# Hyena's projection as three rounded products, its input split on GpSimd during DeltaNet's scan

## What is computed

```
u_l = modulate(x, ...) @ w_in            # columns 800 to 1568 are Hyena's
def hyena_mixer(u_lat, ...):             # 3 * 256 channels, latent tokens only
    uc = short_conv(u, conv_w, conv_b)   # 3 taps, per channel
    v, x1, x2 = split(uc)
    h = hyena_filters(...)               # 3 sine layers of a small network
    z = x1 * long_conv(v, h[0], d[0])
    return x2 * long_conv(z, h[1], d[1])
y = concatenate([gla, hyena, mamba, deltanet]) @ w_out
```

## Time and profile before

| | before |
|---|---|
| median of 3 runs (lowest, highest) | 1843.62 us (1841.35, 1844.65) |
| profiled execution | 1845.53 us |
| its span, first to last instruction | 1843.7 us |
| PE matmul busy | 1596.1 us (87%) |
| DVE busy | 1158.8 us (63%) |
| ACT busy | 880.6 us (48%) |
| POOL busy | 316.5 us (17%) |
| mean granted TensorE clock | 0.931 of 2.4 GHz |

### The profile page before, as it was taken

One profiled execution on the slowest core, in us unless ns is written; L12 is line 12 of the kernel. 1 busy time (PEld: TensorE's weight loads), 2 busy tenths in 40 slices (PEclk: granted clock), 3 DMA queues, 4 the chain that ended last, 5 costly groups with the idle time before them and its releaser, 6 DMA issues. The chain is left out here.

```text
span 1843.7 us, 20249 instructions
## 1 busy us (share of the span) xinstructions
PE 1596.1 (87%) x7651; PEld 1159.2 (63%) x7651; DVE 1158.8 (63%) x1329; ACT 880.6 (48%) x1210; POOL 316.5 (17%) x388
## 2 busy tenths in 40 slices
PE   5899999978998869999888699429999999999981
PEld 2454665457556658954358578328888888888861
DVE  3640552238354655663579723678888888888863
ACT  4240334334426546632110244318777777777752
POOL 0000320045002768110000044101001001101001
PEclk9889999988998979999898899659999999999986
DMA  9740200041003743330220432329999999999957
GB/s 375 244 168 1 92 1 0 0 144 41 0 1 104 235 120 87 98 103 0 69 90 3 172 116 92 154 106 385 380 400 397 384 397 392 381 402 398 380 196 205
DMA packets 101847, 337.02 MB, mean 183 GB/s; under 512 B 36167, under 2 KB 40906, under 8 KB 77047
## 3 DMA queue, kind: packets, MB, share of 16 engines
q1 hardware_dynamic: 91870, 310.89, 44.7%
q0 software_dynamic: 5328, 18.88, 4.2%
q10 hardware_dynamic: 4553, 5.97, 1.2%
HBM read 300.47 MB, written 35.23 MB: 182 GB/s over the span
## 5 line engine op out<-in xcount | busy, mean ns | idle before, releaser
L3116 DVE TENSOR_TENSOR w_lo<-w_raw,w_hi 128x2048 fp32r<-128x2048 f32 x192 | 438.4, 2291 | 65.4 <-ACT w_hi L3058 65.1
L3058 ACT ACTIVATE w_hi<-w_raw 128x2048 fp32r<-128x2048 f32 x192 | 368.0, 1917 | 144.3 <-PE ps L3008 134.1
L540 PE MATMUL ps<-hT,w_mixer 128*128 128x512 f32 (+1 forms) x768 | 313.1, 568 | 5.3 <-PEq L187 3.6
L540 PEld LDWEIGHTS ps<-hT,w_mixer 128*128 128x128 f32 x768 | 147.6, 194 | 159.4 <-issue 155.5
L3006 PE MATMUL ps<-w_hi,xsT_hi 128*128 128x512 f32 x512 | 202.9, 396 | 2.4 <-DVE xsT_lo L3121 2.4
L3008 PE MATMUL ps<-w_hi,xsT_lo 128*128 128x512 f32 x512 | 200.4, 391 | 0.0
L3007 PE MATMUL ps<-w_lo,xsT_hi 128*128 128x512 f32 x512 | 200.2, 391 | 0.0
L3006 PEld LDWEIGHTS ps<-w_hi,xsT_hi 128*128 128x128 f32 x512 | 96.8, 189 | 22.0 <-DVE xsT_lo L3121 2.8
L2974 POOL DMA_INDIRECT moe_sum<-y,idx_col x15 | 30.5, 2037 | 460.6 <-ACT y L3078 460.6
L3008 PEld LDWEIGHTS ps<-w_hi,xsT_lo 128*128 128x128 f32 x512 | 96.5, 189 | 20.4
L3007 PEld LDWEIGHTS ps<-w_lo,xsT_hi 128*128 128x128 f32 x512 | 96.8, 189 | 19.3
(11 more groups left out here) (501 smaller groups left out, 2868.6 us busy)
## 6 DMA issues: line engine op xcount, KB each, us to landing
w_raw<-in_moe_w_gate SPq DMA_DIRECT2D x64, 1024.0 KB, 7.0
w_raw<-in_moe_w_up SPq DMA_DIRECT2D x64, 1024.0 KB, 8.8
w_raw<-in_moe_w_down SPq DMA_DIRECT2D x64, 1024.0 KB, 8.9
w_mod_row<-in_w_mod SPq DMA_DIRECT2D x32, 512.0 KB, 5.0
w_mod<-in_w_mod SPq DMA_DIRECT2D x8, 1024.0 KB, 14.2
w_mixer<-in_w_in SPq DMA_DIRECT2D x4, 2048.0 KB, 11.8
dn_ma<-dn_ma SPq DMA_DIRECT2D x16, 512.0 KB, 3.7
dn_mT<-dn_ma SPq DMA_DIRECT2D x20, 256.0 KB, 3.4
```

Of the source, the lines that this page charges most:

```text
L540: last = nc.tensor.matmul(S.ps[:, 3 * (i % 2) + c, 0:n], S.w[:, k, b["col"]:b["col"] + P], S.hT[:, k, t0:t0 + n], start=(x == 0), stop=(x ...
L3058: nc.scalar.activation(wh[q % RING][:, :], S.raw[q % RAW][:, :], ACT.Copy).then_inc(s.hi, 1)
L3116: nc.vector.tensor_tensor(wl[q % RING][:, :], S.raw[q % RAW][:, :], wh[q % RING][:, :].bitcast(F32), ALU.subtract).then_inc(s.lo, 1)
```

## The change

Hyena's projection is computed in three rounded products. The weights of a block are split by ACT (high part, into spare columns of `w_mixer`) and DVE (low part, in place); the input is split once, by GpSimd at the end of its list in `dn_s`. The low part takes the input's place. The high part needs 8 blocks of 4 KB in each partition: two are new space, two lie in the context part of `hT`, and four in blocks 0, 1, 4 and 5 of `yT`, whose contents are stored to DRAM (`y_kept`) in `dn_s` and loaded back in `hy_f`. The new space comes from the tables: they lose the masks that no instruction reads, and six of the seven levels of each direction's level masks. The diff, cut to its core:

```diff
@@ def tables():
-        tabs["neg_" + name] = ((1.0 - m) * -BIG).astype(f)
-    levels = [] ...
-    tabs["levels_f"] = np.stack(levels, 1).reshape(P, -1)
-    tabs["levels_b"] = np.stack([m.T for m in levels], 1).reshape(P, -1)
+    far = ((j // 64 == c // 64) & (j // 32 != c // 32) & (j > c)).astype(f)
+    tabs["level_f"], tabs["level_b"] = far, far.T
-    tabs["dn_bd"] = (j // HV == (q % P) // HV).astype(f)
-    tabs["half"] = (j // HV == np.arange(2)[None, :]).astype(f)
@@ def project_conv(...):
+        QUARTERS = (0, 2, 3, 1)
+
+        def w_high(i, k):
+            return S.w_low[:, k, HY_COLS + P * (i % 2):HY_COLS + P * (i % 2) + P]
+
+        def split_high(act, i):
+            for j in QUARTERS if i == 0 else (None,):
+                if i == 0:
+                    act.wait_ge(weights[j], 16)
+                ks = slice(0, KD) if j is None else slice(2 * j, 2 * j + 2)
+                col = blocks[i]["col"]
+                nc.scalar.activation(w_high(i, ks), S.w[:, ks, col:col + P], ACT.Copy).then_inc(s.w_hi, 1)
+
+        def split_low(dve, i):
+            for x, j in enumerate(QUARTERS if i == 0 else (None,)):
+                dve.wait_ge(s.w_hi, x + 1 if i == 0 else i + 4)
+                ks = slice(0, KD) if j is None else slice(2 * j, 2 * j + 2)
+                col = blocks[i]["col"]
+                nc.vector.tensor_tensor(S.w_low[:, ks, col:col + P], S.w[:, ks, col:col + P], w_high(i, ks).bitcast(F32),
+                                        ALU.subtract).then_inc(s.w_lo, 1)
+
+        def rounded(pe, i, c, out):
+            ...
+            for x, k in enumerate([2 * j + e for j in QUARTERS for e in range(2)]):
+                if c == mine[i][0] and (i == 0 and k % 2 == 0 or x == 0):
+                    pe.wait_ge(s.w_lo, x // 2 + 1 if i == 0 else i + 4)
+                high = S.h_high[k][:, a0:a0 + 2, :]
+                low = S.h_low[:, k, t0:t0 + 512].rearrange("p (a b) -> p a b", a=2)
+                nc.tensor.matmul(out, w_high(i, k), high, start=(x == 0), stop=False)
+                nc.tensor.matmul(out, w_high(i, k), low, start=False, stop=False)
+                last = nc.tensor.matmul(out, S.w_low[:, k, col:col + P], high, start=False, stop=(x == KD - 1))
@@ tensor
+                    if weights:
+                        last = rounded(pe, i, c, S.ps[:, 3 * (i % 2) + c, :])
@@ scalar
+            if weights:
+                split_high(act, 0)
             norm.act(s, act)
...
             for i, b in enumerate(blocks):
+                if weights and i + 1 < NB:
+                    if i >= 1:
+                        act.wait_ge(s.prod, base[i])
+                    split_high(act, i + 1)
@@ vector
+            if weights:
+                split_low(dve, 0)
             norm.dve(s, dve, ch)
             side.start_dve(s, dve, ch)
             for i, b in enumerate(blocks):
+                if weights and i + 1 < NB:
+                    split_low(dve, i + 1)
@@ dn_s, sync
             for d in range(2):
                 load_blocks(sp, 1, d)
+            for j, b in enumerate(KEPT):
+                sp.dma_start(A["y_kept"][j], S.yT[:, b, :]).then_inc(s.y_kept, 16)
             for st in range(2, T):
@@ dn_s, gpsimd
+            pool.wait_ge(s.y_kept, 16 * len(KEPT))
+            for k in range(KD):
+                raw = S.hT[:, k, CTX:TOK].rearrange("p (a b) -> p a b", a=4)
+                nc.gpsimd.tensor_copy(S.h_high[k], raw).then_inc(s.h_hi, 1)
+                pool.wait_ge(s.h_hi, k + 1)
+                nc.gpsimd.tensor_tensor(S.h_low[:, k, CTX:TOK].rearrange("p (a b) -> p a b", a=4), raw,
+                                        S.h_high[k].bitcast(F32), ALU.subtract).then_inc(s.h_lo, 1)
@@ hy_f, sync, behind the loads of dft_fwd
+            for j, b in enumerate(KEPT):
+                sp.dma_start(S.yT[:, b, :], A["y_kept"][j]).then_inc(y_back, 16)
@@ hy_d, sync, at the end
+            sp.wait_ge(y_back, 16 * len(KEPT))
+KEPT = (0, 1, 4, 5)
```

More of the change, by code:

```diff
@@ L77, in tables @@
         wide["gafter_" + name] = (tabs["after_" + name] / GLA_TAU).astype(f)
-    levels = []
-    s = 1
-    while s < P:
-        m = ((j // (2 * s) == c // (2 * s)) & (j // s != c // s) & (j > c)).astype(f)
-        levels.append(m)
-        s *= 2
-    tabs["levels_f"] = np.stack(levels, 1).reshape(P, -1)
-    tabs["levels_b"] = np.stack([m.T for m in levels], 1).reshape(P, -1)
+    far = ((j // 64 == c // 64) & (j // 32 != c // 32) & (j > c)).astype(f)
+    tabs["level_f"], tabs["level_b"] = far, far.T
     gbd = (j // GLA_DK == np.arange(DG)[None, :] // HV).astype(f)
     wide["gla_bd"] = gbd
-    q = np.arange(DG)[None, :]
-    tabs["dn_bd"] = (j // HV == (q % P) // HV).astype(f)
-    tabs["half"] = (j // HV == np.arange(2)[None, :]).astype(f)
     def packed(ts):
@@ L468, in project_conv @@
     lo = [LAT_AT if x else CTX_AT for x in lat]
-    with Stage(nc, name, "zeroed prod evac centre conv_ch conv_done tok_t tok_e cm_done "
+    with Stage(nc, name, "zeroed prod evac centre conv_ch conv_done tok_t tok_e cm_done w_hi w_lo "
                          + side.sems + norm.sems) as s:
@@ L523, in to_tokens @@
                 last.then_inc(s.tok_t, 1)
+        QUARTERS = (0, 2, 3, 1)
[16 more added lines that the diff above has]
+        def rounded(pe, i, c, out):
+            out = out.rearrange("p (a b) -> p a b", a=2)
+            t0 = chunks[c][0]
+            a0 = (t0 - CTX) // CTX
+            col = blocks[i]["col"]
+            for x, k in enumerate([2 * j + e for j in QUARTERS for e in range(2)]):
[6 more added lines that the diff above has]
+                last = nc.tensor.matmul(out, S.w_low[:, k, col:col + P], high, start=False, stop=(x == KD - 1))
+            return last
         @s.block.tensor
@@ L535, in _ @@
                         norm.free(s, pe, 3 * (i % 2) + c)
-                    order = (0, 1, 4, 5, 6, 7, 2, 3) if weights else range(KD)
-                    for x, k in enumerate(order):
-                        if weights and i == 0 and c == mine[0][0] and k % 2 == 0:
-                            pe.wait_ge(weights[k // 2], 16)
+                    if weights:
+                        last = rounded(pe, i, c, S.ps[:, 3 * (i % 2) + c, :])
+                    for k in range(0 if weights else KD):
                         last = nc.tensor.matmul(S.ps[:, 3 * (i % 2) + c, 0:n], S.w[:, k, b["col"]:b["col"] + P],
-                                                S.hT[:, k, t0:t0 + n], start=(x == 0), stop=(x == KD - 1))
+                                                S.hT[:, k, t0:t0 + n], start=(k == 0), stop=(k == KD - 1))
                     last.then_inc(s.prod, 1)
@@ L1743, in deltanet @@
     with Stage(nc, "dn_s", "p5 p_sb pd tb dt rhs y yc z zc dz x tr wt ws vn qo ke kv s_new av o_out zero taken sub d_st chain "
-                           "pchain") as s:
+                           "pchain y_kept h_hi h_lo") as s:
         Pm = [plan.take(f"dn_p{d}", [P, HEADS, P]) for d in range(2)]
@@ L2010, in masked @@
                 dve.wait_ge(s.p5, n + 1)
-                off = S.t("levels_" + "fb"[d])[:, 5 * P:6 * P]
+                off = S.t("level_" + "fb"[d])
                 nc.vector.tensor_tensor(Pm[d][:, :, :], S.ps[:, b, :].rearrange("p (h c) -> p h c", c=P),
@@ L2374, in forward @@
             yield r, last
-    fwd_in = nc.alloc_semaphore("hy_fwd_in")
+    fwd_in, y_back = nc.alloc_semaphore("hy_fwd_in"), nc.alloc_semaphore("hy_y_back")
     with Stage(nc, "hy_f", "tables turn_in d_in folded taps tapped first skipped mixed even odd copied turned added_even "
@@ L2677, in _ @@
             result(1)
-    SPENT.extend([fwd_in, win_in] + S.hy_w)
+    SPENT.extend([fwd_in, win_in, y_back] + S.hy_w)
 HALF_AT = 32
+KEPT = (0, 1, 4, 5)
 def project_out(nc, S, A):
@@ L3238, in program @@
     S.tab = plan.take("tables", [P, tab.shape[1]])
+    S.spare_at = plan.at
+    plan.at += 8192
     S.pcols = plan.take("param_cols", [P, 69])
@@ L3259, in program @@
     S.w = plan.take("w_mixer", [P, KD, WCOLS])
+    S.h_low = nc.alloc_sbuf_tensor_at("hT_lo", [P, KD, TOK], F32R, offset=S.hT_at)
+    high = [nc.alloc_sbuf_tensor_at(f"hT_hi{k}", [P, 4, 256], F32R, offset=at) for k, at in
+            enumerate([S.spare_at, S.spare_at + SEQ * 4] + [S.yT_at + b * SEQ * 4 for b in KEPT])]
+    S.h_high = [x[:, :, :] for x in high] + [S.h_low[:, 4 * j:4 * j + 4, 0:CTX] for j in range(2)]
+    S.w_low = nc.alloc_sbuf_tensor_at("w_mixer_lo", [P, KD, WCOLS], F32R, offset=S.hT_at + KD * TOK * 4)
     S.stage_at = plan.at
@@ L3325, in declare @@
     A["moe_sum"] = nc.dram_tensor("moe_sum", (SEQ, D), F32, kind="Internal").ap()
+    A["y_kept"] = nc.dram_tensor("y_kept", (len(KEPT), P, SEQ), F32, kind="Internal").ap()
     A["out"] = nc.dram_tensor("out_0_dram", (1, SEQ, D), F32, kind="ExternalOutput").ap()
```

## The result

| | before | changed |
|---|---|---|
| median (lowest, highest) | 1843.62 us (1841.35, 1844.65) | 1831.43 us (1827.78, 1836.63) |
| profiled execution's span | 1843.7 us | 1828.7 us |
| ratio of the times, 95% interval | | 0.9932, 0.992 to 0.9945 |

The change makes the kernel faster by 12.2 us by the medians of five runs each. A second set of five runs, taken later on (e11_after_again), gave 1834.4 against 1844.97 (ratio 0.9953, 0.9939 to 0.9967), 10.6 us. The forecast was 15.0 less, 1828.6. The two profiled executions lie exactly 15.0 us apart, but that is chance, as will be seen.

What follows compares the result with a forecast made beforehand. PE was taken to bound Hyena's projection stage. Stage -12.8, tables -2.5 and GpSimd's sharing with DVE +0.3 sum to -15.0 us, so 1828.6 us against the median of 1843.6; range 1825.5 to 1834.5.

Steps and rivals of the forecast that it cites:

- PE bounds the stage; a cheaper matmul counts in full: Hyena's projection lasts as long as PE's instructions, so cheaper matmuls save their full difference unless something new makes PE wait.
- the prediction's sign of being wrong: PE's idle time before a block's first product named after DVE's weight split, or the barrier before the projection awaiting GpSimd.
- 2.96 us a block: Projection blocks: 48 rounded matmuls at 0.2267 us, 10.88 us instead of 13.84; -14.8 us for blocks 1 to 5.
- The first block, +2.0 (+0.8 to +3.2): Projection's block 0: weight splits delay DeltaNet's norm, PE idles about 3 us, block 1 starts 2.0 us later.
- Splits of later blocks hidden: Projection blocks 1 to 5: splits keep ahead of PE, cover 1.5 to 3 us; rival of late splits 0.08.
- GpSimd's split of the input costs nothing; 0.3 for sharing with DVE: DeltaNet's scan: GpSimd splits the input in idle time, done at 773 to 797 us; DVE's waits cost 0.3 us.
- The rival of a GpSimd that ends the scan: Barrier before the projection waits for GpSimd if a pair costs over 8.9 us; 1852.8 us at 10; chance 0.04.
- Stores and loads back cost nothing: Four finished blocks, 2.1 MB, stored in a pause of SP's queue and loaded back later: nothing, stores at most 5.2 us.
- The tables, -2.5: First stage, bound by bytes: 1.05 MB less at 402 GB/s saves 2.5 us (0 to 2.6); no-gain rival 0.07.
- The sum, -15.0: Whole kernel: projection stage -12.8, tables -2.5, sharing with DVE +0.3, giving 1828.6 us against the median; chance 0.70.

Runs made afterwards that it cites:

- e11_after_again: The changed kernel run again with no edit, a second set of five runs: 1834.4 us, ratio 0.9953 to the kernel before.
- e2_norm_first: Changed kernel with ACT's and DVE's split of block 0's last weight quarter moved behind the norm's first operations: 1829.09 us, ratio to before 0.9914.
- e8_halves: The kernel of e2_norm_first with GpSimd's product of gate and weight in two halves of 1024 elements: 1825.43 us, ratio to before 0.9908.
- e7_split_dear: Changed kernel with three more DVE operations ahead of the low part of blocks 2 and 4: PE waits 1.6 and 0.9 us, `hy_c` 95.8 us.
- e6_pool_late: Changed kernel with three needless GpSimd additions for each of the eight parts of the input's split: 1854.29 us, ratio to before 1.006.
- e4_stores_twice: Changed kernel with each of the four stores of finished outputs issued twice, to different places in DRAM: 1831.53 us, scan 138.3 us.

## Why the prediction was right, and where it was off

**PE bounds the stage; a cheaper matmul counts in full**: right. No block but the first waits for anything new. By its letter the prediction's sign of being wrong, PE's idle time before a block's first product named after DVE's split, did come, at block 0; but there it was priced: PE starts 0.95 us after the stage's start, as reckoned (0.9), instead of at once.

**2.96 us a block**: the mechanism was right, the size off by 0.25. From block 1 to the next stage it took 902.68 - 819.79 = 82.89 us before and 888.69 - 819.30 = 69.39 after, so -13.5 for five blocks, not -14.8. The pace is 0.2319 us and not the experts' 0.2267. Of the 0.25 us, 0.11 are the first gap of a block (0.34 or 0.32 us), which stands behind fp32 transposes or the filter's products and which the 37 rows of the experts didn't contain; 0.14 are the other gaps above 0.227, up to 0.241, their cause open. The 216 ns of the Trainium skill ("TensorE: Matmul & The Clock Gate", Back-to-back issue gap), which the page calls the gap of an isolated matmul, would have been further off still: by it a block is an estimated 10.4 us, against 11.1 measured.

**The first block, +2.0 (+0.8 to +3.2)**: +3.3, since block 1 starts 819.79 - 799.73 = 20.1 us after the stage's start before and 23.4 after. The step was right in kind: the norm stands behind the last quarter, its product stands behind GpSimd, PE idles. Three sizes were off. The norm began 5.9 us late, not 5.1, as the quarter landed 5.1 us after the stage's start and not at the least landing of the earlier trace rows. PE's block 0 was done 13.5 us after the start, 0.7 sooner than reckoned, so the idle time is 4.4 and not 3; 0.5 of that is a slip in the reckoning (at 0.43 us each only 9 matmuls are done by 804.6, and the other 39 end at 813.4, not 813.9). And the clock fell, which I had left open and weighed by half: 3.49 us for the transposes is 1.6 more, not 2.4. Here the prediction had also misread a row: 0.65 from 900 to 901 us means a fall at 900.3 and not at 900.7. e2_norm_first and e8_halves show this cause by taking it away: the two edits together give back 5.3 us.

**Splits of later blocks hidden**: right, and with the cover that I had reckoned (1.5 to 3 us); e7_split_dear measures it as 2.0 and 2.8.

**GpSimd's split of the input costs nothing; 0.3 for sharing with DVE**: right in the main. A part takes 3.43 us, just under my range of 3.6 to 6.6, and the last ended at 767.6 instead of 773 to 797, since GpSimd also came to it at 739.9 and not at 744.2. Two L2088 were lengthened, as foreseen, by 1.8 us together; the scan was not longer for it, and not in e6_pool_late either, where eight were. The Trainium skill's rule ("SBUF — State Buffer", SBUF: two separate sides) that GpSimd and a DVE operation with two SBUF inputs exclude each other is borne out where it touches the path: 0.43 us became 3.20 in e2_norm_first. The rival of a GpSimd that ends the scan is right as a mechanism (e6_pool_late), and its condition was not met.

**Stores and loads back cost nothing**: right for the stores (e4_stores_twice). The loads back were not tried by themselves, but the stretch that holds them is not longer than before (see the sum).

**The tables, -2.5**: the step that failed. I priced all 1.05 MB at the 402 GB/s of the earlier trace rows. The last piece starts only 1.4 us earlier (means of three and eleven profiles), because from 4 to 12 us the DMA engines, as busy as before, moved less; what slowed them no run shows. GLA's first product comes 1.2 us earlier, and the times give 0.4 (between 2.0 less and 1.5 more). A fall of PE's clock in a piece, which then needs 0.8 to 1.6 us more, in seven profiles of eleven and one of three, blurs every comparison of this stage.

**The sum, -15.0**: the parts as measured are -10.2 for `hy_c`, -0.4 to -1.2 for the first stage, and perhaps -1 behind `hy_c`, which I can't assign to the change: from `hy_f`'s first product to the experts' first it is 331.3 to 331.8 us in three profiles of fp32 projections and 329.3 to 331.7, on average 330.6, in the eleven of rounded ones. Together some -12; the two sets of runs have 12.2 and 10.6. Against the forecast, blocks 1 to 5 gave 1.3 us too little, the first block cost 1.3 too much, and the tables gave 1.3 to 2.1 too little; what came behind `hy_c` made up for some of it. The 15.0 of the two profiled spans are the measured parts, with some 3 us of luck ahead of the projection: from GLA's first product to the scan's first it was 601.7 us before and 599.4 after, but 601.7 and 599.1 in the two profiles of the kernel before alone. So the forecast of 1828.6 was 3 us too low, in its range, and its direction was never in doubt.

## What to carry to other kernels

When an engine's list starts with a wait for a late DMA, everything behind it inherits the lateness, here a norm that needs nothing of that DMA: put the work that is ready ahead of it, and look at what the moved piece then stands behind. A long GpSimd instruction on two SBUF inputs stops a short DVE one beside it; two halves let it through. Bytes saved in a stage that waits for DMAs need not be worth their time at the stage's average rate: look at the GB/s of the very microseconds in which they moved, and price the saving by a run of that part alone.

## What the hardware showed

The first stage, with the same instructions, let GLA's first product start 54.6 to 57.5 us into the execution in eleven profiles. A good part of this is TensorE's clock in two bursts: eight matmuls took 1.91 us or up to 3.53, at a granted clock of 1.00 or 0.52 over two microseconds, and the 16 of L388 took 2.0 to 3.4. A single pair of profiles can thus differ by 3 us ahead of any change; here luck of this size made the forecast look exact.

DMA engines that are busy nearly all the time can move a fifth less: 318 GB/s from 4 to 8 us (busy share 0.98) with tables of 450 KB on ACT's queue beside SP's loads, 406 (1.00) with tables of 1475 KB.

After 4.4 us without work PE's transposes ran at 0.50, though the record of the idle time itself (811 to 813 us) still reads 1.00 and that of 813 to 814 us 0.86:

```profile
811.00:813.00 2.00, 0.00 (x0) 0.00 (x0) 1.97 (x2) 0.00 (x0) 0.00 (x0) 1.00 0.02 4
```
